# Output products of the second tile moved up between the last two levels of a chunked recurrence

## The reference

```python
def hgrn2_chunkwise(q, k, log_f, v):            # 8 heads, DK = DV = 128
    def step(state, chunk):
        qc, kc, lfc, vc = chunk
        cum = jnp.cumsum(lfc, axis=2)
        o_inter = jnp.einsum('bhtk,bhkv->bhtv', qc * jnp.exp(cum), state)
        ...
        scores = jnp.einsum('bhtsk,bhsk->bhts', qc[:, :, :, None, :] * decay, kc)
        o_intra = jnp.einsum('bhts,bhsv->bhtv', scores, vc)
        ...
        state = jnp.exp(last)[..., None] * state + jnp.einsum('bhsk,bhsv->bhkv', k_to_end, vc)
        return state, o_inter + o_intra

    o = rms_norm_2(hgrn2_chunkwise(qf, kf, log_f, vf), hg_norm)
    y_b = o.reshape(B_, S_, HG_HEADS * HG_DV).astype(h.dtype) * jax.nn.silu(g)
    y = jax.nn.sigmoid(m_a) * y_a + jax.nn.sigmoid(m_b) * y_b
    return y @ w_out
```

## Time and profile before

| | |
|---|---|
| median of 3 runs | 2765.17 us (2764.44 to 2766.04) |
| the profiled execution | 2764.83 us, its span 2763.0 us |
| mean granted TensorE clock | 0.994 |
| TensorE busy | 2678.8 us, 97% of the span |
| VectorE, ScalarE, GpSimd busy | 1654.1, 1021.6, 993.8 us |
| last level of the last head to the next stage's first product | 1978.10 to 2010.93 us of the span |

### The profile page before, as it was taken

One profiled execution on the slowest core, in us unless ns is written; L12 is line 12 of the kernel. 1 busy time (PEld: TensorE's weight loads), 2 busy tenths in 40 slices (PEclk: granted clock), 3 DMA queues, 4 the chain that ended last, 5 costly groups with the idle time before them and its releaser, 6 DMA issues.

```text
span 2763.0 us, 39753 instructions
## 1 busy us (share of the span) xinstructions
PE 2678.8 (97%) x16338; PEld 2199.8 (80%) x16338; DVE 1654.1 (60%) x1823; ACT 1021.6 (37%) x1394; POOL 993.8 (36%) x604
## 2 busy tenths in 40 slices
PE   7999999999999999999999999999899999999997
PEld 4887777888788888788888888888777888888885
DVE  6498128886954456555546666666769443444436
ACT  4432217773433343444552222222334222222222
POOL 0233115103488864222221111111143744445552
PEclk9999999999999999999999999999999999999999
DMA  7111440022321223111121111111022111121112
GB/s 235 63 38 39 154 152 1 1 77 77 122 61 46 61 85 107 54 46 46 46 57 47 39 39 39 39 39 39 24 84 69 51 41 57 50 62 54 54 31 99
DMA packets 260432, 174.79 MB, mean 63 GB/s; under 512 B 5792, under 2 KB 252960, under 8 KB 259104
## 3 DMA queue, kind: packets, MB, share of 16 engines
q1 hardware_dynamic: 258816, 169.69, 20.4%
q10 hardware_dynamic: 1440, 2.59, 0.3%
HBM read 163.87 MB, written 8.39 MB: 62 GB/s over the span
## 4 chain that ended last, share of the span: by engine, by line
PE 68%; issue 14%; DVE 9%; POOL 4%; ACT 3%; DVEq 2%; DMA 0%; POOLq 0%; SPq 0%; ACTq 0%
PE PS L2601 10%; PE PS L2603 10%; PE PS L2602 10%; PE PS L2189 10%; PE PS L2191 9%; PE PS L2190 9%; POOL Wlo L616 3%; DVE acol L1732 1%; ACT exp L1039 1%; DVE qR L1680 1%; PE PS L2705 1%; PE PS L2712 1%; PE PS L2287 1%; PE PS L2512 1%; PE PS L2741 1%
## 5 line engine op out<-in xcount | busy, mean ns | idle before, releaser
L616 POOL TENSOR_TENSOR Wlo<-Wraw,Whi 128x1024 fp32r<-128x1024 f32 (+1 forms) x140 | 342.2, 2445 | 1090.1 <-ACT Whi L817 1090.1
L2189 PE MATMUL PS<-Bh,Whi 128*128 128x512 f32 x1216 | 486.0, 400 | 7.6 <-DVE Bl L1471 3.4
L2191 PE MATMUL PS<-Bh,Wlo 128*128 128x512 f32 x1216 | 474.8, 390 | 0.0
L2190 PE MATMUL PS<-Bl,Whi 128*128 128x512 f32 x1216 | 474.1, 390 | 0.0
L2189 PE MATMUL PS<-Hh,Whi 128*128 128x512 f32 x672 | 267.4, 398 | 12.3 <-POOL Wlo L616 6.9
L2189 PEld LDWEIGHTS PS<-Bh,Whi 128*128 128x128 f32 x1216 | 228.6, 188 | 61.6 <-DVE Bl L1471 7.4
L2191 PEld LDWEIGHTS PS<-Bh,Wlo 128*128 128x128 f32 x1216 | 228.4, 188 | 49.0
L2190 PEld LDWEIGHTS PS<-Bl,Whi 128*128 128x128 f32 x1216 | 228.8, 188 | 45.5 <-issue 0.7
L2191 PE MATMUL PS<-Hh,Wlo 128*128 128x512 f32 x672 | 262.1, 390 | 0.0
L2190 PE MATMUL PS<-Hl,Whi 128*128 128x512 f32 x608 | 237.1, 390 | 0.0
L817 ACT ACTIVATE Whi<-Wraw 128x1024 fp32r<-128x1024 f32 (+1 forms) x140 | 144.5, 1032 | 129.4 <-PE PS L2191 127.0
(11 more groups left out here) (454 smaller groups left out, 5875.4 us busy)
## 6 DMA issues: line engine op xcount, KB each, us to landing
Wraw<-in_w_in SPq DMA_DIRECT2D x64, 512.0 KB, 4.1
adaV<-in_ada_w SPq DMA_DIRECT2D x16, 1024.0 KB, 5.2
Wraw<-in_odd_w_in SPq DMA_DIRECT2D x32, 512.0 KB, 4.5
Wraw<-in_w_up SPq DMA_DIRECT2D x32, 512.0 KB, 4.0
Wraw<-in_w_down SPq DMA_DIRECT2D x28, 512.0 KB, 4.3
Wraw<-in_even_w_in SPq DMA_DIRECT2D x24, 512.0 KB, 3.7
adaW<-in_ada_w SPq DMA_DIRECT2D x8, 1024.0 KB, 11.3
Wraw<-in_even_w_out SPq DMA_DIRECT2D x14, 512.0 KB, 3.9
```

Source lines behind the costliest of these rows:

```text
L616: pool.tensor_tensor(Wlo[:, slot, 0:tiles, :], Wraw[:, slot, 0:tiles, :], Whi[:, slot, 0:tiles, :].bitcast(F32), ALU.subtract).then_inc(lo ...
L2189: mm(out, Whi[:, u % 2, k, :], hi[:, k, c], start=(k == 0), stop=False)
L2190: mm(out, Whi[:, u % 2, k, :], lo[:, k, c], start=False, stop=False)
L2191: return mm(out, Wlo[:, u % 2, k, :], hi[:, k, c], start=False, stop=(k == KT - 1))
```

## The change

`both(1)` moves from behind the keys' turn of the last head to between level 5 and level 6. Each of the following places gets the next tile: `both(2)` stands behind the keys' turn, `both(3)` behind the increments, `both(4, 5)` behind the output rows and `both(6)` behind the output turn. `both(7)` stays. No other engine's program is changed.

```diff
         level(last, 4)
         both(0)
         level(last, 5)
+        both(1)
         level(last, 6)
         keys_turn(last)
-        both(1)
+        both(2)
         increments(last)
-        both(2)
+        both(3)
         output_rows(last)
-        both(3, 4)
+        both(4, 5)
         output_turn(last)
-        both(5, 6)
+        both(6)
         both(7)
         by_halves(2, o0, (Bh, Bl))
```

## The result

The changed kernel takes 2770.14 us (median of 20 executions, 2768.77 to 2772.97) against 2765.12 us before (20 executions, 2764.27 to 2766.50): +5.0 us, a ratio of 1.0019 with a 95% interval of 1.0013 to 1.0025. It is slower, by an amount just inside the 0.2% that was set as the line. The forecast was 2770.7 in a range of 2768.9 to 2773.0. The profiled execution took 2770.26 (span 2768.4), 5.43 above that of before.

What follows compares the result with a forecast made beforehand. TensorE, with 68% of the chain, was taken to bound the kernel through its gaps. Increments 5.55 us later, less a small gain at the end, gave +5.5 on 2764.83, 2770.3; plus 0.34 for the median, 2770.7, range 2768.9 to 2773.0.

Steps and rivals of the forecast that it cites:

- Tile 1 isn't there: Between levels 5 and 6, `both(1)` waits for VectorE's low part of tile 1 until 1983.24, a wait of 8.2 us.
- a sign of being wrong: Any product of tile 1 starting before 1983 on TensorE would show the forecast wrong.
- `both(1)` at the low clock: Ahead of level 6, its 12 products take 2.85 us plus a surcharge of 1.7 for running at 1.2 GHz at first.
- Level 6 and the keys' turn warm: Behind `both(1)`, these two TensorE steps run at the high clock, taking 1.07 and 0.85 us.
- The increments 5.55 us later: In the last head, the increments start at 1992.8 instead of 1987.24.
- The other reading of the sum: Ahead of the increments: TensorE idles 3.0 us more, does one more tile (2.85), loses some 0.3 less to the low clock.
- Slack of VectorE, 2 us: Ahead of the increments' end near 1994.5, VectorE is free with tile 3 done at 1992.3, so no charge.
- From the increments to the output turn, 13.66: This stretch keeps its order with other tile numbers and its 13.66 us, if VectorE keeps up.
- The end gives back 0.16, less 0.08: Behind the output turn, one tile fewer starts `both(7)` 0.16 us earlier, less 0.08 for a first product following a wait.
- The shift runs through to the end: The whole delay passes through later stages; a change of over 1 us there would show the forecast wrong.
- The second gap cools the clock: Rival: the new 2.4 us wait behind `both(6)` lowers the clock at `both(7)`; +7.0 us in all, 2772.2; chance 0.24.
- the first rival: The rival of a cooled clock behind the new 2.4 us wait ahead of `both(7)`: 2772.2 us, chance 0.24.

Runs made afterwards that it cites:

- e4: Changed kernel with VectorE making tile 1's low part behind level 4's copy, nine instructions earlier: 2768.55 us, +3.3 against the kernel before.
- e1: Changed kernel with `both(4)` alone ahead of the output turn and `both(5, 6)` behind it: 2769.65 us, +4.4 against the kernel before.
- e6: Changed kernel with 33 useless matmuls between level 5 and `both(1)` to hold the clock up: 2768.64 us, +3.4 against the kernel before.
- e7: Kernel before with 12 useless matmuls in each of its waits, ahead of level 6 and of the keys' turn: 2764.12 us, −1.1.
- e2: Kernel before with only its end changed, `both(3, 4, 5)` ahead of the output turn and `both(6)` behind it: 2768.75 us, +3.5.
- e3: Changed kernel with `both(1)` between level 6 and the keys' turn: 2770.27 us, +5.0 against the kernel before.
- e9: e4 with tile 2's low part also made earlier, right behind the keys' product on VectorE: 2766.46 us, +1.1 against the kernel before.
- e5: Kernel before with VectorE's keys' product ahead of the queries' product in the last head, tile 1's low part right behind: 2764.57 us, −0.7.

## Why the prediction was right

The direction, the size and the mechanism came out as forecast; what was off are two terms of the sum. Point by point:

- **Tile 1 isn't there.** Right. Wait for `Bl` L2024 of 8.16 us (8.2 forecast); it ends 0.06 us behind the product on VectorE (0.15 assumed). e4 shows that this is the cause: with tile 1 made early the wait is 1.14 us, and D falls from +5.76 to +2.2. By the clock of the record tile 1's first product began at 1982.70, ahead of the 1983 that was named as a sign of being wrong. It was not early: the record is 0.60 ahead at tile 0's product already.
- **`both(1)` at the low clock, 4.55 us, 4.65 with the step into level 6.** It was 5.06. This is the term that was mis-sized: the low clock lasted 4.4 us (1982.70 to 1987.10), and 5.0 in e1, where the two rows of before had 2.99 and 3.9. I took the middle of two rows for a quantity that the executions scatter more widely: surcharges of 2.1 here, 2.5 in e1 (where the whole of `both(1)` ran at 1.2 GHz, the upper bound that was given as 2.4), none in e6 with the clock held up.
- **Level 6 and the keys' turn warm.** Right: 1.08 and 0.84 (1.07 and 0.85 forecast).
- **The increments 5.55 us later.** Counted from tile 0's product, 22.72 against 16.83: 5.89. The 0.3 too much is the clock term. The other reading of the sum, that the change "loses some 0.3 less to the low clock" than before, does not hold as a price: by e6 and e7 the low clock costs the changed kernel 2.1 and the kernel before 1.1. In the kernel before level 6 was slow (1.79 us), but VectorE's keys were not there yet anyway, so that part cost nothing.
- **Slack of VectorE, 2 us.** Right: 2.21 idle ahead of the increments' sums.
- **From the increments to the output turn, 13.66.** 13.67.
- **The end gives back 0.16, less 0.08.** From the output turn to `both(7)` were 6.36 us, now 6.09, so 0.27 came back; with the slower step behind a wait the next stage's first product stands 9.89 behind the turn instead of 10.03, 0.14. The wait that was forecast as 2.4 is 2.33. One tile fewer behind the turn is no gain in itself (e2: the turn comes 2.7 later and a wait of 2.29 takes the place of the work), and leaving two there would have given back 0.9 (e1). I did not see that second part: `both(4, 5)` ahead of the turn covers 1.15 us more than the norm needs.
- **The shift runs through to the end.** The span grew by 5.4, D by 5.76; 0.60 of offset was there before tile 0. The remainder of 0.2 lies behind the next stage's first product, within the 1 us allowed; what it is made of is open. That the growth of the record, 5.4, is so near to the sum of 5.5 is in part luck: the stretch that the sum is about grew by 5.76, and the offset hid the difference.
- **The second gap cools the clock.** Not in the profiled execution, but in e2, e3 and e9, at waits of 2.29 to 2.33 us. So it happens in some executions. From `both(7)` to the next stage it cost 0.65 (e2), 0.67 (e3) and 1.28 us (e9), less than the 1.5 of the forecast, as in e2 and e3 the first three products still ran at 2.4 GHz. It would widen the spread, and the changed kernel's executions do spread over 4.2 us where those of before spread over 2.2; that this is the reason is argued, not shown.
- **The medians.** The sum was 5.5; the records gave 5.43, the medians 5.02. I added the whole distance of one record (0.34) to the median of three; with 20 executions each the median of before is 2765.12, and the changed one's profiled execution lay above its own median (2770.26 against 2770.14). So most of the half us lies between record and median, not in a step. The forecast also put the line of 0.2% at a surcharge of 1.7; the surcharge was 2.1, and the loss of the medians stayed under the line all the same. The half us decided on which side of 0.2% the result fell: the forecast had it on the line and leant to the wrong side.

## What to carry to other kernels

A piece of work moved ahead of a wait only fills it if its own input is there earlier: look in the producer's program for the place at which the input is made, not only at the time at which it could be. On an engine that works in order, a filler that comes late is worse than the wait that it should fill, since everything behind it, with its data ready, waits too; then each later slot gets the next tile, and the input of that one has to be looked up as well (e4).

A cover that is moved from one slot to another should be compared with what each slot can hide: here the slot ahead of the output turn was 1.5 us too short with one tile and too long by 1.2 with two.

## What was not expected of the hardware

The length of the low clock is not a constant of the program. From the keys' turn on, with TensorE's order and the wait ahead of it (2.27 and 2.09 us) nearly unchanged, it was 2.99 us in the record of before and 5.6 us in e2, and the time from the turn to the increments differed by 1.3 us with it. Behind the wait of 8.16 and 8.15 us it was 4.40 us in the changed kernel and 4.98 in e1.

Waits as short as 2.29, 2.32 and 2.33 us ahead of `both(7)` (e2, e3, e9) were followed by 1.2 GHz, while waits of 2.32 and 2.33 us at the same place (e6, the changed kernel and e4) were not. The row at 424.27 of the earlier trace rows, on which the first rival rested, is of this kind too. In the record of the changed kernel the same wait had the same length, and the clock stayed high:

```profile
425.38 0.48 PE L2512 MATMUL PS<-kT,qT 64*128 64x256 f32 x1 [2.49 <-ACT exp L1039]
...
426.60:429.80 3.20, 3.20 (x26) 2.45 (x23) 2.95 (x5) 1.91 (x2) 3.06 (x2) 1.00 0.00 0
```

Over the twelve records this wait lasted 2.49 or 2.50 us each time; the clock fell behind it in six (before, e1, e3, e4, e5, e6) and not in the other six, though nothing ahead of it was edited. So for waits of 2.3 to 2.5 us one record says nothing about the next execution.

Products with no use, issued only to bridge the waits, took 2.1 us off the path in the changed kernel's record (e6) and 1.1 us in that of the kernel before (e7).
